# The first half of gate1's modulation matmuls, ahead of or behind the S5 chunk sums on TensorE

## What is computed

```python
mod = silu(cond) @ w_ada + b_ada            # six rows of 1024: shift1 scale1 gate1 shift2 scale2 gate2
h = rms_norm(x, norm1_g) * (1 + scale1) + shift1
proj = h @ w_in                             # 768 columns to S5, 256 to the Fourier mixer
y_s5, final_state = s5_mixer(proj[..., :768], ...)   # two directions, 48 groups, 64 complex states
y_f = fourier_mixer(proj[..., 768:], w_fnet)
x = x + gate1 * (concat(y_s5, y_f) @ w_out)
h2 = rms_norm(x, norm2_g) * (1 + scale2) + shift2
x = x + gate2 * moe(h2, ...)                # 32 experts, top 4, w_gate, w_up, w_down 4 MB each
y = rms_norm(x, norm_f_g)
```

## Time and profile before

| | us |
|---|---|
| runs | 1115.11, 1117.52, 1118.09 |
| median | 1117.52 |
| profiled execution, own time | 1117.14 |
| its span in the profile | 1115.3 |
| TensorE matmul busy | 925.5 (83%) |
| VectorE busy | 338.9 (30%) |
| ScalarE busy | 240.2 (22%) |
| moved by DMA | 451.55 MB, mean 405 GB/s |

### The profile page before, as it was taken

The page is one execution under the profiler, slowest core; times in us unless marked ns, Lnnn a source line. Parts: engine busy times, 40 slices in busy tenths (PEclk is TensorE's granted clock), DMA queues, the critical chain, the costliest instruction groups (busy, mean ns, idle before and its releaser), DMA issues.

```text
span 1115.3 us, 32114 instructions
## 1 busy us (share of the span) xinstructions
PE 925.5 (83%) x13926; PEld 565.1 (51%) x13927; DVE 338.9 (30%) x819; ACT 240.2 (22%) x401; POOL 29.1 (3%) x29
## 2 busy tenths in 40 slices
PE   3899699699997878998878879999967999696964
PEld 1577474455554535554545445555533555353532
DVE  7889932322221212221211212222211221121213
ACT  4464722212221111221111111211111221121111
POOL 2001112100000000000000000000000000000000
PEclk8999799699998988999988989999988999898997
DMA  9748999899999999999999999999999999999996
GB/s 380 321 152 322 341 342 397 344 431 431 431 429 435 429 435 427 438 427 434 432 431 432 430 429 428 431 432 432 431 432 432 432 428 432 426 439 425 438 424 228
DMA packets 22224, 451.55 MB, mean 405 GB/s; under 512 B 3146, under 2 KB 3658, under 8 KB 5082
## 3 DMA queue, kind: packets, MB, share of 16 engines
q1 hardware_dynamic: 21450, 450.28, 95.9%
q10 hardware_dynamic: 432, 0.57, 0.2%
q0 software_dynamic: 320, 0.39, 0.2%
HBM read 448.27 MB, written 2.18 MB: 404 GB/s over the span
## 4 chain that ended last, share of the span: by engine, by line
PE 51%; DMA 33%; DVE 12%; issue 3%; ACT 1%; DVEq 0%; ACTq 0%; SPq 0%
PE ps L950 22%; DMA pair<-in_w_down 17%; PE ps L979 13%; DMA pair<-in_w_up 11%; DMA ring<-in_w_down 4%; PE ps L609 3%; PE ps L886 3%; PE ps L833 2%; PE ps L686 2%; DVE scan_w L1386 2%; PE ps L820 1%; DVE acts L1543 1%; DVE upc L1539 1%; DVE upc L1536 1%; DVE actT L1547 1%
## 5 line engine op out<-in xcount | busy, mean ns | idle before, releaser
L950 PE MATMUL ps<-pair,XT 128*32 128x256 f32 x6528 | 404.1, 403 | 70.6 <-DMA pair<-in_w_gate 38.6
L950 PEld LDWEIGHTS ps<-pair,XT 128*32 128x32 f32 x6528 | 223.9, 116 | 220.1 <-DMA pair<-in_w_gate 40.5
L979 PE MATMUL ps<-pair,actT 128*32 128x256 f32 x1600 | 100.6, 408 | 22.6 <-DMA pair<-in_w_down 21.6
L1534 DVE TENSOR_SCALAR gcl<-ps 128x256 f32<-128x256 f32 x51 | 21.7, 425 | 273.9 <-PE ps L950 273.9
L979 PE MATMUL ps<-ring,actT 128*32 128x256 f32 x1664 | 96.0, 381 | 3.6 <-DMA ring<-in_w_down 2.0
L1536 DVE TENSOR_SCALAR upc<-ps 128x256 f32<-128x256 f32 x51 | 21.7, 425 | 249.9 <-PE ps L950 249.9
L1219 ACT COPY selT<-ps 128x256 f32<-128x256 f32 x51 | 19.0, 372 | 330.9 <-PE ps L609 330.9
L979 PEld LDWEIGHTS ps<-pair,actT 128*32 128x32 f32 x1600 | 56.5, 117 | 60.6 <-issue 31.4
L979 PEld LDWEIGHTS ps<-ring,actT 128*32 128x32 f32 x1664 | 51.0, 110 | 42.2 <-DVE actT L1547 7.7
L1216 ACT ACTIVATE sgm<-gcl 128x256 f32<-128x256 f32 x51 | 21.3, 417 | 213.3 <-DVE gcl L1534 213.3
L1216 ACT ACT_TABLE_LOAD x51 | 65.4, 1283 | 3.1 <-DVEq L1497 2.3
(11 more groups left out here) (252 smaller groups left out, 758.2 us busy)
## 6 DMA issues: line engine op xcount, KB each, us to landing
pair<-in_w_gate SPq DMA_DIRECT2D x32, 4096.0 KB, 29.5
pair<-in_w_up SPq DMA_DIRECT2D x32, 4096.0 KB, 35.0
pair<-in_w_down SPq DMA_DIRECT2D x16, 4096.0 KB, 38.4
ring<-in_w_down SPq DMA_DIRECT2D x32, 2048.0 KB, 39.0
ring<-in_w_ada SPq DMA_DIRECT2D x11, 2048.0 KB, 9.5
wout<-in_w_out SPq DMA_DIRECT2D x1, 4096.0 KB, 19.7
w<-in_w_in SPq DMA_DIRECT2D x2, 1536.0 KB, 21.7
wglu<-in_w_glu SPq DMA_DIRECT2D x1, 2304.0 KB, 12.0
```

The source lines that it names most:

```text
L950: ins = pe.matmul(out[32 * fq:32 * fq + 32, :], XT[:, k % 2, (k // 2) * 32:(k // 2) * 32 + 32], tile_of(turn, m, k)[:, fq * QU:(fq + 1) * ...
L979: ins = pe.matmul(pY[32 * dq:32 * dq + 32, :], actT[:, k % 2, (k // 2) * 32:(k // 2) * 32 + 32], tile_of(turn, 2, k)[:, dq * QU:(dq + 1) * ...
```

## The change

The call `mod_half(2, 0)` and the wait in front of it move from ahead of the chunk sums to behind them, directly in front of `mod_half(2, 1)`. Nothing else is touched: SyncE's queue, the homes of the halves and the order on the other engines are as they were.

```diff
-            pe.wait_ge(bank_drained[6], 1)
-            mod_half(2, 0)
             pe.wait_ge(sem("U_ready"), 3)
             pe.wait_ge(sem("GT_ready"), 12)
             pe.wait_ge(sem("bb_ready"), 1)
...
                             if n == 7:
                                 full(ins)
 
+            pe.wait_ge(bank_drained[6], 1)
+            mod_half(2, 0)
             mod_half(2, 1)
             mod_half(3, 0)
             pe.wait_ge(sem("wfn_in"), 16)
```

## The result

| | before | after |
|---|---|---|
| median of the runs, us | 1117.66 (4 runs) | 1134.41 (4 runs) |
| lowest and highest | 1115.11, 1118.09 | 1133.03, 1135.10 |
| profiled execution, own time | 1117.14 | 1134.68 |
| its span | 1115.3 | 1132.9 |

The ratio is 1.0159, with a 95% interval of 1.0146 to 1.0172. The change costs 16.8 us, where +7.9 us (1125) was forecast with a range up to 1129. The direction was right, and the forecast was 9.4 us too low.

A forecast was written before the change was run, and what follows sets the result against it. The expert weight stream, gapless from 216 us, bounds the kernel, its start set by the chain before 191 us. Terms: 0 (steps 1 and 2) + 8.4 + 1.6 - 2.1 = +7.9, giving 1125 us, range 1119.5 to 1129.

The forecast's parts named there:

- Direction and chain: Slower: late half (3,0) delays `uf`, ScalarE's queue, line 786 and so the expert weight stream; slower given 0.82.
- Step 1: Line 719 on TensorE, no longer behind the moved matmuls, starts near 70.8 instead of 72.73 us, 1.9 us earlier.
- Step 2: Low clock falls on line 719 instead; its end taken as unchanged at 83.9 us, bounds -0.9 and +0.4.
- rival C: Clock stays low longer: line 719 ends 1.9 us later, `uf` loses 2 us more; 1129 us, chance 0.10.
- the skill's rule: Transposes don't release the clock, so chunk sums would begin at 1.2 GHz, the +0.4 side; set aside from the trace.
- Step 3: Half (3,0) waits in SyncE's queue for the moved half: TensorE starts it 8.4 us late, then 1.6 us slower.
- ScalarE's room of 2.1 us: ScalarE's state copies before line 786 absorb 2.1 us of lateness: 1.45 us idle plus 0.66 us ahead of VectorE.
- The end of the chain: Line 786's +7.9 us passes in full to `o3`, expert 1's down issue at 208.03 us, and the end.
- A: Line 719's gain is kept, the late transfer never reaches the scan; 1116.5 us; 0.15 shared with B, faster 0.03.
- B: T copies, not ScalarE, bound line 786; +0.9 to +3.1 us, 1118.4 to 1120.6; 0.15 shared with part of A.

The follow-up runs named there:

- late_transfer: Kernel before plus one SyncE wait, so half (3,0) and those behind it are issued only when the chunk sums are done; 1121.92 us, ratio 1.0062.
- late_act_order: `late_transfer` with ScalarE's copies of states 8 moved ahead of its copy of `yf`; 1121.32 us, ratio 1.0046 to the kernel before.
- fill: Changed kernel with 16 dense matmuls on constants in the old place of `mod_half(2, 0)`, transfer of half (3,0) still late; 1124.25 us, ratio 1.0070.
- fill_own: Changed kernel with dense matmuls on constants ahead of the chunk sums and half (3,0) in a tile of its own; 1116.73 us, ratio 0.9999.
- split: Kernel before with `mod_half(2, 0)` cut in two, half ahead of the wait for `uc`, half behind the U transposes; 1116.41 us, ratio 0.9994.
- full_rows: Changed kernel with chunk sums contracted over 128 rows instead of 64, outputs not those of the layer; one timed execution of 1153.94 us.
- uc_gap: Kernel before with all of `mod_half(2, 0)` moved ahead of the wait for `uc`; 1124.92 us, ratio 1.0073.
- interleave: Changed kernel with `mod_half(2, 0)` moved forward to behind the first two of the twelve chunk-sum banks; 1120.83 us, ratio 1.0038.

## Why the prediction was wrong, step by step

**Direction and chain: right.** The kernel is slower, the expert stream is delayed as a whole, and the chain goes through the transfer of half (3,0), `uf`, ScalarE's queue and line 786, as predicted.

**Step 1, the start of the chunk sums: right.** They start 0.1 us after the last U copy ends, at 71.59 us against the 70.8 of the text plus the 1.0 us by which this execution was late there already.

**Step 2, the clock: this step failed.** It took the rise of the clock as a matter of when, with an end of line 719 between -0.9 and +0.4 us of before, and +1.9 in rival C. Measured: +8.1, of which 1.0 is the early shift. The mechanism was named (the low stretch falls on line 719) and the term mis-sized: it was put at 0 and measured at +7.1, because line 719 does not bring the clock back at all. The estimate of 0.10 us per record at the low clock was good (0.107 measured). What was wrong was how many records get it: 24 to 55, 90 in rival C, and in fact all but the first few of 192. The error is in the choice of the neighbouring row. Line 786 took the clock back after 5.5 us and looks alike (192 records, 64 moved columns), but it has 128 rows and 64 weight columns, where line 719 has 64 rows and 128 weight columns, and its records take 0.053 us at the low clock against 0.107. The kernel before has no row in which line 719 runs from the low clock for more than half a microsecond, so its behaviour there was unmeasured. The upper bound should have been that it never lifts it: 192 x (0.10 - 0.058) = 8.1 us, less 1.9.

The low stretch itself was read from one execution. In the kernel before the clock fell at 69.9 us, under `mod_half(2, 0)`; in `late_transfer`, which has the same order on TensorE up to there, it did not fall at all, nor in `late_act_order`, `fill`, `fill_own` and `split`. So what the moved matmuls do for the chunk sums is not to take a fixed low stretch in their place: with them right ahead the chunk sums have the full clock, but for the first half microsecond in the kernel before; in the six profiles without them there it fell, by 2.7 us into the chunk sums at the latest.

The transposes of `h_tok`, on which I set the skill's rule aside, are no firm row either: they took 3.30 us in the kernel before, where the clock rose under them, and 3.31 in `full_rows`, but 3.65 to 3.68 us in the other ten profiles; in the changed kernel it stood at 0.50 to their end and rose only behind them. The rule (the Trainium skill, "TensorE: Matmul & The Clock Gate", Part 4: PE-mode transpose) says that transposes do not engage the full clock. As the prediction used it, the chunk sums would have begun at the low clock; in the changed kernel and in `uc_gap` they began at the full clock and lost it 0.4 and 2.7 us in. The price that the text gave to that side, +0.4, was the wrong number in either case.

**Step 3, the transfer: right in kind and nearly in size.** Issued right behind the moved half, it landed after 7.5 us (8.5 had been assumed); TensorE waited 5.26 us (6.4) and ran the half in 3.33 us (3.53); `uf` lost nothing (0 taken, and up to 1.2 us in `fill`: 8.33 us instead of 7.17). But the moved half itself took 3.6 us at the low clock instead of 1.9.

**ScalarE's room of 2.1 us: right.** `uf` ends 18.65 us late, line 786 starts 16.7 us late: 1.95 us were absorbed. `late_transfer` was forecast at +5.7 by the same step and measured at +5.7, though its interval allows +4.6 to +9.2.

**The sum with measured terms.** The chunk sums end 8.1 us late. From there to `mod_half(3, 0)` it was 2.1 us before (83.92 to 85.98, the matmuls of half (2,1)) and is 11.2 now (92.04 to 103.22: 3.6 for the moved half, 7.6 for the transfer). So it starts 8.1 + 11.2 - 2.1 = 17.2 us late. With 1.4 for its low clock and 2.0 of room that is +16.6 at line 786. The span moved by 17.6.

**The end of the chain: nearly right.** A late microsecond at line 786 is a late microsecond at the end within about one: line 786 starts 16.7 us late, the down halves of expert 1 are issued 15.8 us late, and the span is 17.6 us longer. But it is not the issue of the down halves of expert 1 alone that sets the stream, as the text had it. `split` issued them 3.2 us earlier and gained 1.0. The landing of `w_gate` of expert 2 is the better mark: span less that landing is 884 us in the kernel before (1115.3 - 231.3) and 885 in the changed one (1132.9 - 247.9), and that issue hangs on the first expert round, whose own clock varies between executions.

**Rivals.** A and B did not occur. C was the right kind, with a price of 3.9 us above the forecast where about 9 were needed.

## What to carry to other kernels

Before moving dense matmuls away from a wait, ask what behind them holds or lifts the clock in their place: a stream that keeps the full clock once it has it need not be able to win it back, and unless a row of the trace shows that very stream at the low clock, its bound is the whole stream at the low clock. Read the queue that refills the tile of moved work, since a later reader is a later transfer for everything behind it in that queue. And when a change has two effects in series, put each right alone and then both: four numbers show the size of each, and the fourth that nothing else is left within its interval.

## What the runs showed of the hardware

The chunk sums (64 rows, 128 weight columns, 64 moved columns) hold the clock at 2.4 GHz when a dense stream runs right up to them (10.94 to 11.16 us in five kernels: `fill`, `fill_own`, `late_transfer`, `late_act_order`, `split`) or in the middle of them (`interleave`). Behind transposes and a gap of 1.1 us they did not hold it, though they had it at their start: they lost it after 0.4 us in the changed kernel and after 2.7 us in `uc_gap`, and then stayed at 1.2 GHz to their end, 20 us in the changed kernel and 15.3 in `uc_gap`. The same instructions with 128 moved columns had the full clock 3.5 us after their start. I had expected every steady stream of matmuls to bring it back in a few microseconds. At the low clock they take 0.107 us per record against 0.057, nearly twice; contracting over 128 rows instead of 64 takes twice as long again, 0.215 us. The Trainium skill ("TensorE: Matmul & The Clock Gate", Part 1: The HAM clock gate) says that the throttled state is the default and that activity releases it. The runs agree with that as far as `mod_half` goes, where the clock came back 3.0 to 4.9 us after a stretch of dense matmuls had begun (`interleave` and `uc_gap`), and show a stream that is busy without a gap in the profile and doesn't do it. Which property of the stream decides stays open: more moved columns were enough in the one execution that tried them, more rows also halved the pace, and the pace of the weight loads was not varied by itself.
